# Experts ranked by load, four at 128 rows paired with four at 64 rows

## The reference

```python
def _swiglu(h, w_gu, w_down):
    gu = h @ w_gu                                # 1024 x 7168 per expert
    f = w_gu.shape[-1] // 2                      # 3584
    return (jax.nn.silu(gu[..., :f]) * gu[..., f:]) @ w_down    # 3584 x 1024

def _moe(h, router_w, w_gu, w_down):
    logits = t @ router_w
    top_v, top_i = lax.top_k(logits, 2)
    gates = jax.nn.softmax(top_v, axis=-1)
    for e in range(8):
        out = out + combine[:, e:e + 1] * _swiglu(t, w_gu[e], w_down[e])
```

## Time and profile before

| | us |
|---|---|
| median of three executions | 1980.46 |
| the profiled execution: span, which is also its time in the list | 1979.3 |
| from the first expert product to the end of the span | 974.8 |
| TensorE busy | 1913.8 (97% of the span) |
| VectorE busy | 1570.8 (79%) |
| ScalarE busy | 1262.1 (64%) |
| read from HBM | 501.19 MB |

### The profile page before, as it was taken

The page is one execution under the profiler, slowest core; times in us unless marked ns, Lnnn a source line. Parts: engine busy times, 40 slices in busy tenths (PEclk is TensorE's granted clock), DMA queues, the critical chain, the costliest instruction groups (busy, mean ns, idle before and its releaser), DMA issues.

```text
span 1979.3 us, 29550 instructions
## 1 busy us (share of the span) xinstructions
PE 1913.8 (97%) x10607; PEld 1584.8 (80%) x10608; DVE 1570.8 (79%) x1836; ACT 1262.1 (64%) x1767; POOL 159.4 (8%) x119
## 2 busy tenths in 40 slices
PE   6999999999999998999999999999999999999997
PEld 5976888888888876777877888888888888888885
DVE  3166458655667976988689999999999999999998
ACT  4245562222465454656577888888888888888885
POOL 1000000000001243544000000000000000000100
PEclk9999999999999998999999999999999999999999
DMA  9374235655455320222569999999999999999994
GB/s 357 114 264 163 86 121 178 210 194 191 149 182 185 108 62 28 87 69 92 199 244 360 363 392 380 371 388 363 394 364 387 378 370 387 364 393 372 377 395 192
DMA packets 248783, 508.34 MB, mean 257 GB/s; under 512 B 10651, under 2 KB 63211, under 8 KB 248683
## 3 DMA queue, kind: packets, MB, share of 16 engines
q1 hardware_dynamic: 246256, 499.60, 70.0%
q0 software_dynamic: 1856, 6.82, 0.9%
q10 hardware_dynamic: 571, 0.57, 0.1%
HBM read 501.19 MB, written 5.77 MB: 256 GB/s over the span
## 4 chain that ended last, share of the span: by engine, by line
PE 80%; DVE 11%; ACT 3%; issue 3%; DMA 2%; POOL 1%; ACTq 0%; DVEq 0%; SPq 0%; POOLq 0%
PE bank L856 19%; PE bank L858 18%; PE bank L857 18%; PE bank L1121 4%; PE bank L1123 4%; PE bank L1122 4%; DVE ar L2586 3%; DVE lo L2208 2%; PE bank L1221 1%; PE bank L1222 1%; PE bank L1223 1%; PE bank L887 1%; PE bank L1498 1%; PE bank L863 1%; ACT ar L1684 1%
## 5 line engine op out<-in xcount | busy, mean ns | idle before, releaser
L2208 DVE TENSOR_TENSOR lo<-raw,hi 128x1024 fp32r<-128x1024 f32 x844 | 1016.5, 1227 | 207.8 <-ACT hi L1621 142.3
L1639 ACT ACTIVATE hi<-raw 128x1024 fp32r<-128x1024 f32 x672 | 710.0, 1063 | 178.0 <-PE bank L858 172.7
L856 PE MATMUL bank<-hi,xh_t 128*128 128x512 f32 (+1 forms) x1184 | 447.8, 378 | 4.8 <-DVE lo L2208 3.7
L858 PE MATMUL bank<-hi,xl_t 128*128 128x512 f32 (+1 forms) x1184 | 444.8, 376 | 0.0
L857 PE MATMUL bank<-lo,xh_t 128*128 128x512 f32 (+1 forms) x1184 | 444.5, 375 | 0.0
L1621 ACT ACTIVATE hi<-raw 128x1024 fp32r<-128x1024 f32 x130 | 137.4, 1061 | 259.2 <-PE bank L1123 172.6
L856 PEld LDWEIGHTS bank<-hi,xh_t 128*128 128x128 f32 x1184 | 223.4, 189 | 48.7 <-issue 6.6
L858 PEld LDWEIGHTS bank<-hi,xl_t 128*128 128x128 f32 x1184 | 223.3, 189 | 40.4
L857 PEld LDWEIGHTS bank<-lo,xh_t 128*128 128x128 f32 x1184 | 223.4, 189 | 39.1
L856 PE MATMUL bank<-hi,hth 128*128 128x512 f32 x624 | 248.3, 398 | 3.1 <-DVE lo L2208 3.1
L858 PE MATMUL bank<-hi,htl 128*128 128x512 f32 x624 | 243.3, 390 | 0.0
(11 more groups left out here) (368 smaller groups left out, 2238.7 us busy)
## 6 DMA issues: line engine op xcount, KB each, us to landing
raw<-in_moe_gu_w_dram SPq DMA_DIRECT2D x224, 1024.0 KB, 7.8
raw<-in_moe_down_w_dram SPq DMA_DIRECT2D x112, 1024.0 KB, 7.5
raw<-in_ada_w_dram SPq DMA_DIRECT2D x14, 2048.0 KB, 8.9
raw<-in_ffn_gu_w_dram SPq DMA_DIRECT2D x22, 1024.0 KB, 5.0
raw<-in_ffn_down_w_dram SPq DMA_DIRECT2D x22, 1024.0 KB, 4.8
ar<-in_ada_w_dram SPq DMA_DIRECT2D x20, 1024.0 KB, 5.1
raw<-in_ssm_in_w_dram SPq DMA_DIRECT2D x16, 1024.0 KB, 5.2
raw<-in_mix_out_w_dram SPq DMA_DIRECT2D x8, 1024.0 KB, 7.2
```

The lines of the kernel that those rows point to most:

```text
L856: mm(o, a_hi, w_hi, start=first, stop=False, **kw)
L858: return mm(o, a_lo, w_hi, start=False, stop=last, **kw)
L1639: A_(hi[:, p % SPL, :], raw[:, u, (p % 2) * PIECE:(p % 2 + 1) * PIECE], ACT.Copy).then_inc(m_hi, 1)
L2208: TT(lo[:, p % SPL, :], raw[:, u, h * PIECE:(h + 1) * PIECE], hi[:, p % SPL, :].bitcast(F32), ALU.subtract).then_inc(done, 1)
```

## The change

1. The experts are ranked by the number of their tokens. Ranks 0 to 3 are "heavy": 128 rows, as before, three fp32r products. Ranks 4 to 7 are "light": at most LIGHT_CAP = 64 rows, and TensorE takes the raw float32 weights as they landed, without a split. The 64 columns of the stationary operand fill half of the array, so two matmuls are put side by side in two column tiles (`tile_position=(0, 64 * half)`), one for each 512 columns of a piece. A heavy expert with over 128 tokens, or a light one with over 64, gets a second pass at the end. Expert 0 is always rank 0.
2. Heavy and light experts are paired (0 with 4, and so on) and run together: two heavy units, then two light units that lie four units (M_LAG = 4) further back. The whole stream is written out; there is no hardware loop over experts.
3. The hidden width is cut in steps of 1024, 1024, 1024 and 512 columns (FCOLS), not seven of 512. A gate or up unit is now 2 x 128 rows by 1024 columns, 4 KB runs, but for the last step, which keeps 4 x 128 by 512.
4. The slot ring stays at six. A transfer waits for `m_lo` where a heavy unit was in the slot, for `l_used` (TensorE has used the unit) where a light one was.
5. The expert results no longer go through memory: no `moe_rows`, no indirect transfers. Gathering (`gather_heavy`, `gather_light`) and combining (`combine_heavy`, `combine_light`) are matmuls with selection matrices, for each pair. The weights' addresses are read from a register (`sp.value_load(ids ...)`); the rank is computed by some dozen small VectorE operations before the first split.

```diff
+HEAVY = N_EXPERTS // 2
+LIGHT_CAP = 64
+FCOLS = (1024, 1024, 1024, 512)
+M_LAG = 4
+def expert_stream():
+    units = []
+    for p in range(HEAVY):
+        for s in range(FSTEPS):
+            units += [(p, "g", s, i) for i in range(gu_units(s))]
+            units += [(p, "u", s, i) for i in range(gu_units(s))]
+            if s > 0:
+                units += [(p, "d", s - 1, i) for i in range(4)]
+            elif p > 0:
+                units += [(p - 1, "d", LAST, i) for i in range(2)]
+    return units + [(HEAVY - 1, "d", LAST, i) for i in range(2)]
+for _n in range(0, NSTREAM + M_LAG, 2):
+    if _n < NSTREAM:
+        LOADS += [("h", _n), ("h", _n + 1)]
+    if _n >= M_LAG:
+        LOADS += [("l", _n - M_LAG), ("l", _n - M_LAG + 1)]
...
+            for i, (kind, n) in enumerate(LOADS):            # SyncE
+                if i < RAW:
+                    sp.wait_ge(lo_ready, 2 * (S_MOE + i - RAW + 1))
+                elif LOADS[i - RAW][0] == "h":
+                    sp.wait_ge(m_lo, 2 * LOADS[i - RAW][1] + 2)
+                else:
+                    sp.wait_ge(l_used, LOADS[i - RAW][1] + 1)
+                main_load(i, role[(kind, p)], k, s, j)
...
+            def light_unit(l):                               # TensorE
+                    for t in range(nt):
+                        c = nt * j + t
+                        for half in range(2):
+                            m = mm(bank[3][64 * half:64 * half + 64, 0:n], xL[p % 2][:, c, :],
+                                   w[:, t, half * n:(half + 1) * n],
+                                   start=(c == 0), stop=(c == KC - 1), tile_position=(0, 64 * half))
+                m.then_inc(l_used, 1)
+            def combine_light(p, b, o):
+                pe.wait_ge(yl_evac, p + 1)
+                for half in range(2):
+                    r = slice(64 * half, 64 * half + 64)
+                    mm(o[half][:, :], gT[r, 2 + b, :], yL[r, :], start=False, stop=True).then_inc(cmb_t, 1)
+            def after_heavy(n, p, k, s, i):
+                if (k, s, i) in (("g", 1, 1), ("g", 1, 2)):
+                    turn_heavy(p, 0, i - 1)
+                if (k, s) == ("u", 1) and i in (0, 2) and p > 0:
+                    combine(p - 1, i // 2)
+                if (k, s, i) == ("d", 0, 0) and p < HEAVY - 1:
+                    gather_heavy(p + 1)
...
+            slots(posm, 0)                                   # VectorE
+            lo_main(1)
+            dve.wait_ge(rt_cnt, 1)
+            own(dve.tensor_copy(cntf, bank[3][:, 0:8]))
+            own(STT(key_, cntf, 8.0, iota8, ALU.mult, ALU.subtract))
...
+            dve.tensor_copy(ids[:, :], idsf).then_inc(rank_done, 1)
+            own(TT(prod2, one_r.unsqueeze(1).to_broadcast((P, 2, 8, 8)), posm.unsqueeze(2).to_broadcast((P, 2, 8, 8)), ALU.mult))
+            own(dve.tensor_reduce(pos_r[:, :, :], prod2, AX.X, ALU.add))
+            gather_split(0)
+            lo_main(2)
+            slots_light(0)
+            lo_main(3)
```

More of the change, by code:

```diff
@@ new lines, in heavy_d @@
+            def heavy_d(n, p, s, i):
+                if i == 0 and s == 0:
+                    pe.wait_ge(y_evac, Y_MAIN + 2 * p)
+                for t in range(2):
+                    q, c = 2 * n + t, 2 * i + t
+                    pe.wait_ge(m_lo, q + 1)
+                    if c % 4 == 0:
+                        pe.wait_ge(ht_lo, n_th(p, s, c // 4) + 1)
+                    a = (c % 4) * P
+                    for half in range(2):
+                        m = tok3(bank[half][:, :], hth[:, c // 4, a:a + P], htl[:, c // 4, a:a + P], *mpiece(q, half * 512),
+                                 first=(s == 0 and c == 0), last=(s == LAST and c == 3))
+                    m.then_inc(m_used, 1)
@@ new lines, in turn_heavy @@
+            def turn_heavy(p, s, half):
+                n = n_th(p, s, half)
+                pe.wait_ge(hh_done, n + 1)
+                wait_from(pe, ht_lo, n)
+                if n == 0:
+                    pe.wait_ge(gat_mod, 1)
+                elif s == 1 and half == 0:
+                    pe.wait_ge(*((gat_mod, 2 * p + 3) if p < HEAVY - 1 else (cmb_add, 4 * p)))
+                for q in range(4):
+                    m = pe.transpose(bank[6][:, q * P:(q + 1) * P], hH[:, half * 512 + q * P:half * 512 + (q + 1) * P], ident)
+                m.then_inc(ht_t, 1)
@@ new lines, in gather_heavy @@
+            def gather_heavy(p):
+                pe.wait_ge(slot_ready, 2 * p + 1)
+                if p == 1:
+                    pe.wait_ge(ht_lo, 2)
+                    pe.wait_ge(tl_c, 1)
+                elif p > 1:
+                    pe.wait_ge(cmb_add, 4 * (p - 1))
+                for k in range(KC):
+                    for b in range(2):
+                        m = mm(bank[6 + k // 4][:, (k % 4) * P:(k % 4 + 1) * P], xres[:, b, k * P:(k + 1) * P],
+                               slot1[:, b, :], start=(b == 0), stop=(b == 1))
+                    if k % 4 == 3:
+                        m.then_inc(gat_t, 1)
@@ L1566, in at_step, with combine_rest @@
                         m.then_inc(gs_t, 1)
-                    if j == J_SLOTS + 1 and after:
-                        token_of_slot(it + 1)
-                    if j == J_GATHER and after:
-                        turn_rows(it + 1)
-                moe_swiglu(it, at_step)
-            gather(0)
-            expert(0, None, True)
-            with pe.Fori(1, N_EXPERTS - 1) as e:
-                expert(e, None, True)
-            expert(N_EXPERTS - 1, 0, False)
-            for b in range(2):
-                combine(N_EXPERTS - 1, 0, b)
+                moe_swiglu(e, at_step)
+            def combine_rest(e, b):
+                if b == 0:
+                    pe.wait_ge(gT_ready, HEAVY + e + 1)
+                    pe.wait_ge(y_evac, Y_MOE + 2 * e + 2)
+                for half in range(2):
+                    if b == 1:
+                        pe.wait_ge(cmb_add, A_MOE + 4 * e + half + 1)
+                    mm(bank[2 + half][:, :], gT[:, b, :], yexp[:, half * 512:(half + 1) * 512],
+                       start=True, stop=True).then_inc(cmb_t, 1)
             pe.wait_ge(rt_done, RT_N)
@@ L2107, in gather_mod @@
+            def gather_mod(e):
                 a_, b_ = mod_cols(3, 0)
```

786 lines of the change are left out of this document (537 added, 249 removed).

## The result

| | before | after |
|---|---|---|
| median of the executions, us | 1980.63 (1979.3 to 1981.71) | 1921.07 (1918.65 to 1923.75) |
| the profiled execution: time / span | 1979.3 / 1979.3 | 1923.75 / 1921.9 |
| TensorE busy | 1913.8 (97%) | 1816.8 (95%) |
| VectorE / ScalarE busy | 79% / 64% | 59% / 46% |

The changed kernel takes 0.9697 of the time (95% interval 0.9683 to 0.971), 59.6 us less. The forecast was 1890, in a range of 1868 to 1950: right in sign and in the change of the bound, too low by 31 us. The measured time lies above the 1872 to 1912 that the forecast gave its own mechanism; it is inside the range because the range reaches on to the rivals' 1950.

The account below looks back on a forecast made before the run. TensorE bound the kernel before; the DMA engines would after. Last landing at 1868, 6 us of ring losses, 1.8 for the last light unit and 14.5 to the end sum to 1890.3; forecast 1890 us, range 1868 to 1950.

Parts of the forecast that it names:

- The bound passes from TensorE to the DMA engines: Expert stage, per pair of experts: DMA engines need 217.6 us, TensorE 211.2, so the DMA engines set the pace; chance 0.62.
- Ceiling for 4 KB runs 407 GB/s: Weight stream: the mean of two backlogged windows, 407 GB/s, taken as the DMA rate with 4 KB runs, 2.576 us per unit.
- TensorE's work per pair, 211.2: TensorE, per heavy and light expert: products, transposes, gathering, combining and tile-mode round trips sum to 211.2 us, against 238.7 before.
- A pair every 218 to 220 us: Expected sign in the changed kernel's windows: each pair of experts takes 218 to 220 us.
- 1.5 us lost per pair at the ring: Second step of a pair: combining and gathering delay TensorE until the six-slot ring blocks; 1.5 us lost, bounds 0 and 6.
- The start loses 5 us, once: Start of the expert stage: small VectorE operations and splits ahead of pieces 4 to 6 cost TensorE about 5 us, once.
- After the last landing 1.8 + 14.5: End of the kernel: 1.8 us for the last light unit, then 14.5 us from the last expert product to the end.
- the forecast's own band, 1872 to 1912: Whole kernel: time in us if the DMA engines set the pace as forecast; chance 0.62.
- Rival 1: Expert stage: TensorE stays the bound, with four stops of 3.6 us per pair and clock falls; 1931 us, chance 0.16.
- Rival 2: Weight stream: keeps its present rate whatever the run length; 1934 us at 385 GB/s, 1950 at 378; chance 0.12.
- rival 3: Light products: column tiles don't overlap at 512 columns, a piece costs 1.71 us; kernel 2155 us, slower; chance 0.05.
- rival 4: Light experts: one with over 64 tokens needs a second pass, 119 us and its start more; 2020 us, chance 0.03.

## Why the prediction was right, and where it was too low

- *The bound passes from TensorE to the DMA engines*: right. The waits turned round, 136 us less of TensorE's work bought 10, and a stream at 391 instead of 405 GB/s cost 26.
- *Ceiling for 4 KB runs 407 GB/s*: right, 406 to 407 over stretches of 50 to 185 us, though not throughout, as the forecast's sign had it: at the turns it is 328 to 351. With 2 KB runs in two thirds of the units it is 391. The page DMA: Bandwidth & Descriptors of the Trainium skill (Where 436 GB/s comes from) has the HBM side bind at about 358; the trace of after disagrees as that of before did, with 406.
- *TensorE's work per pair, 211.2*: close. A light record costs (5.37 - 1.94) / 16 = 0.214 instead of 0.219, 1.5 us less per pair; the light gather 3.5 (1020.12 to the next product at 1023.61) instead of 3; the round trips 21 x 0.42 = 8.8 instead of 5. Some 3 us too low, hidden but for the turns. The 0.24 came from products of 128 columns. That a change of tiling mode drains the engine (the Trainium skill, TensorEngine Tiling (Array Packing), Key Properties) agrees in kind with this trace, where a round trip costs 0.42 us for these products.
- *A pair every 218 to 220 us*: wrong. It is 1541.69 - 1317.12 = 224.6, from one gather to the next:

```profile
1317.12 3.73 PE L1666 MATMUL bank<-ar,xres 128*128 128x128 f32 x32
1541.69 3.73 PE L1666 MATMUL bank<-ar,xres 128*128 128x128 f32 x32
```

- *1.5 us lost per pair at the ring*: this is the step that failed first, 21.8 at three turns (24.5 with the stop of open cause) instead of 6 in all, for single pairs (8.7, 7.6) beyond the bound of 6. It weighed work against the ring, but no wait: TensorE's second step was summed as if nothing in it were queued behind something late. In a kernel where the splits wait for landings, all that VectorE has behind a split waits for landings too, which the prediction's own remark that VectorE falls to 56% does not show. Undoing this order gave 11.3 us, one more slot 12.0.
- *The start loses 5 us, once*: too small. TensorE did stop for 1.99 us at 1015.67, behind VectorE's small operations, as the forecast had it. Not forecast were the second stop at 1028.57, behind ScalarE's eight copies, which waited 2.43 us for the gather with hi pieces behind them, and that the stream would run dry. At 1023.5 some ten units had landed, as forecast, but from 1025 to 1030 nothing moved (0 GB/s), where the forecast had two more on their way; the mean up to 1040 was 138 GB/s. The other order of both gave 8.6 of the 10.9.
- *After the last landing 1.8 + 14.5*: the 14.5 holds (1908.27, the end of the last light unit, to 1921.9 is 13.6). The 1.8 was 7.8, since TensorE is not in step at the end: the six light units behind the last heavy one and the heavy combination keep it busy.
- *The range*: the forecast's own band, 1872 to 1912, missed by 9 us. Three terms were too small in the same direction, and the range held only by the room left for rivals that did not come true.
- *Rival 1* (TensorE stays the bound, 1931) was nearest in time and wrong in kind. The half clock behind a stop is there, but at the start and at two of the three turns, not at every step, and the time between the turns follows the stream. *Rival 2* is refuted by the rates, *rival 3* by the spacing and by the kernel with one tile, *rival 4* by an end without a second pass.

## What to carry to other kernels

When a change makes the stream of weights the bound, look through each engine's order for work that others wait for and that stands behind an operation fed by a landing: with ample idle time on the engine it is late all the same, and each such place empties a ring of a few slots. A loss of that kind can be cured from both sides, by order or by one more buffer, and here most of the two gains added up. And price the first and the last units by themselves: here nearly half of the error was there, in 2% of the time.

## What was not expected of the hardware

- Two float32 products of 512 columns in two column tiles overlap whether they alternate or come in twos (3.58 and 3.63 us for 16 records), and not at all within one tile (7.01).
- A round trip between tiled float32 and untiled fp32r products costs 0.42 us.
- The light combining products, 64 rows on two row tiles, overlap as well: four records from 1306.69 on, with the next product 1.06 us later, where four of 128 rows took 1.81.

```profile
1304.88 1.88 PE L1694 MATMUL bank<-ar 128*128 128x512 f32 x4
1306.69 1.13 PE L1701 MATMUL bank<-ar 64*128 64x512 f32 x4
1307.75 0.50 PE L933 MATMUL bank<-hi,xh_t 128*128 128x512 f32 x1
```
